# Three narrow products in place of one wide and one narrow product per weight block, with new places for the split weights

## The chip, the cores and the metric

One core of one Trainium2 chip. The metric is the device time of one execution in microseconds (us), the median of several runs; the kernel before takes 1187.89 us (1187.58 to 1189.35 in 3 runs).

## What is computed

A decoder block of width 1024 over 256 tokens, batch 1, in float32, followed by a second block of another kind. The first has two layers; each is a feed-forward, a mixing step and another feed-forward. Cut to what matters:

```
def swiglu(x, w_gate, w_up, w_down):          # D_MODEL 1024, D_FF 2816
    return (silu(x @ w_gate) * (x @ w_up)) @ w_down

for layer in range(2):
    h = h + 0.5 * swiglu(rms_norm(h, g1), w_gate1, w_up1, w_down1)
    hn = rms_norm(h, mix_norm_g)
    # layer 0: hn @ a_w_in, a causal convolution of 31 taps, layer_norm; memory attention
    # layer 1: hn @ b_w_in, causal attention with 12 heads; memory attention
    h = h + concat(primary, mem_out) @ w_o
    h = h + 0.5 * swiglu(rms_norm(h, g2), w_gate2, w_up2, w_down2)
# second block: rms_norm(h) @ w_in_2 (some 6,700 columns), a differential attention, an mLSTM,
# gates, @ w_a_2, @ w_b_2, @ w_out_2, a norm, and the sum with h
```

There are four feed-forwards, numbered 0 to 3 below. They hold about three fifths of all multiplications.

## The kernel before

**Exact products from rounded ones.** TensorE multiplies in a rounded float32 (`fp32r`). Each operand is therefore split into a rounded part and the rest: a weight w into `whi` + `wlo`, an activation x into `xh` + `xl`. A product is then the sum of three: hi·xh, hi·xl and lo·xh, added up in PSUM.

**Weights in slots.** All weights come in 403 slots of 128 partitions by 1024 values (512 KB), in the order of use. SyncE's queue loads slot i into `raw[i % 7]`; ScalarE writes its rounded half to `whi[i % 5]` (line 1253), VectorE the rest to `wlo[i % 5]` (line 1864). ScalarE may write slot i once TensorE has used slot i - 5 (semaphore `used`). In a slot for columns there are 4 pieces of 128 rows by 256 columns; each piece is two blocks of 128 by 128.

**Three forms of product**, all issued by the helper `mm` (line 509):
- *Wide* (`two_blocks`, feed-forwards alone). The activations are laid out as [piece, hi or lo, 256 tokens], so that xh and xl of a piece lie next to each other. For each block one matmul of 512 columns multiplies hi by [xh | xl] into a whole PSUM bank, and one of 256 columns adds lo·xh to the bank's left half. A pair of blocks (256 output features) takes two banks, and the result is the sum of each bank's two halves. ScalarE copies the right halves to SBUF (`half`, line 1295), VectorE adds the left halves (`halves`, line 1913).
- *Narrow* (`pair` and `direct`, the other matrices whose result has the features on the partitions: slots 72 to 75, 78 to 85, 90 to 97, 258 to 265, 334 to 350, 371 to 394, which are 69 slots). For each block three matmuls of 256 columns, hi·xh, hi·xl and lo·xh, into one half of a bank. Both blocks of a pair share one bank and there is nothing to add up.
- *Rows* (`rows_steps`, `query_rows`). The activations are the stationary operand, and the weights move through TensorE, 512 or 256 columns at a time.

**Order of a feed-forward** (`ffn`). For p = 0 to 10 (256 columns of the hidden layer): the gate product over 8 pieces (2 slots) into banks 0 and 1, then the up product into banks 2 and 3. TensorE waits for `sum` of the pair before, before it overwrites a pair of banks. ScalarE and VectorE follow a slot at a time: right halves, sum, scale by the norm's row (`gate_scale`, line 2006), SiLU, product gate by up (line 2014), and the split of the product into `gh` and `gl` of the tile `g`. Then for p = 0 to 3 the down product over 22 pieces (6 slots) into banks 4 and 5, 6 and 7, 0 and 1, 4 and 5, its sum of halves, the scale, the sum with h, and the split of the new h into the activations of the next step (`prep`).

**Places in SBUF.** This is about a place's address in a partition, modulo 256 bytes. The tiles `whi` and `wlo` begin at one and the same place, called 0 here, and a slot's stride is 4096 bytes, so every block of every slot begins at 0. `activations` makes two views on each tile `x0`, `x1`: `xh`, `xl` begin at +64, `rh`, `rl` at 0. The feed-forwards' and the narrow products' moving operands (`xh`, `xl`) are at +64, and so is the tile `g` of feed-forwards 0, 1 and 3; `g` of feed-forward 2 is at +128. Rows products have rh, rl (0) in the slots 28 to 31, 86 to 89, 234 to 257 and 395 to 402, and xh, xl (+64) in 76, 77 and in 351 to 370.

Of the kernel before, what the change touches and what calls it, by code (L numbers as in the profile page):

```python
# [15 lines left out]
S = 256  # L16
# [16 lines left out]
SLOTS = 403  # L33

# [43 lines left out]
def a_slot(p):  # L78

    return AIN + 4 * p + (2 if p else 0)  # L80

# [113 lines left out]
def buffers(nc, ctx):  # L195
# [9 lines left out]
    B.whi = sb("whi", [128, SPLIT, SLOT], F32R)  # L205
    B.wlo = sb("wlo", [128, SPLIT, SLOT], F32R)
# [3 lines left out]
    B.diag = sb("diag", [128, 2, 128])  # L210
# [21 lines left out]
    B.ln1 = sb("ln1", [128, 128])  # L232
# [36 lines left out]
    A.cv = sb("cv", [128, 6, S], F32, mx)  # L269
    A.sg = sb("sgm", [128, 2, 512], F32, mx)  # L270
# [19 lines left out]
    sb("even", [128, 4], F32, kv)  # L290
# [25 lines left out]
    T.ctap = sb("ctap", [128, 8, 4], F32, mx)  # L316
# [7 lines left out]
    T.ptbuf = sb("pt2", [128, 2, 256], F32, mx)  # L324
    T.lamr = T.ptbuf[:, 0, :].rearrange("p (a d) -> p a d", a=4)
# [8 lines left out]
def signals(nc, ctx):  # L334
# [17 lines left out]
    sums = []  # L352
    for f in range(4):
        for p in range(PAIRS):
            sums += [("gate", f, p), ("up", f, p)]
        sums += [("down", f, p) for p in P4]


# [15 lines left out]
    s.consts = sig("consts", ["ones", "ident", "ln1", "upper", "identb", "mask", "half", "alib", "ident4"])  # L374
# [72 lines left out]
    s.half = sig("right_half", sums)  # L447


    s.sum = sig("halves_sum", sums)  # L450
# [52 lines left out]
def tensor_engine(nc, B, s):  # L503
    pe = nc.tensor
    bank, psum, xh, xl, rh, rl, ident, ones = B.bank, B.psum, B.xh, B.xl, B.rh, B.rl, B.ident, B.ones
# [5 lines left out]
    def weights(i, nk, n):  # L511
        h = B.whi[:, i % SPLIT, 0:nk * n].rearrange("p (k n) -> p k n", k=nk)
        l = B.wlo[:, i % SPLIT, 0:nk * n].rearrange("p (k n) -> p k n", k=nk)
        return h, l
# [15 lines left out]
    def two_blocks(b, h, l, x, start, stop, ready=None):  # L530


        two_rounded(b, h, x, start)
        if ready is not None:
            pe.wait_ge(*ready)
        return two_left(b, l, x, stop)
# [10 lines left out]
    def part(x, slot, b, ks, start, stop, gen=None, between=None):  # L547
# [8 lines left out]
        for i, kc in enumerate(ks):  # L556
            k = kc % 4
            if slot == 0 and i == 2:
                pe.wait_ge(*s.hi.at(0))
            if between and i == 2:  # L560
                between()
            if gen:
                first_use(s.x_hi, gen, kc)
                first_use(s.x_lo, gen, kc)
            if late:
                two_rounded(b, h[:, k, :], x[:, kc], start and i == 0)
            else:
                t = two_blocks(b, h[:, k, :], l[:, k, :], x[:, kc], start and i == 0, stop and kc == ks[-1], ready.get(i))
        if late:
            pe.wait_ge(*s.lo.at(slot))  # L570
            for kc in ks:
                t = two_left(b, l[:, kc % 4, :], x[:, kc], stop and kc == ks[-1])
# [126 lines left out]
    def ffn(f, x, gen):  # L699
        base, F = FFN[f], B.ffn[f]  # L700
        for p in range(PAIRS):
            if f == 0 and p == LATE:
                rows((rh[1], rl[1]), "mem0", 8, MKV0, 512, [[4], [5]])
            if p:
                pe.wait_ge(*s.sum.at(("gate", f, p - 1)))
            elif f == 1:
                pe.wait_ge(*s.h.at((2, 0)))
            elif f == 2:
                pe.wait_ge(*s.h.at((3, 2)))
            elif f == 3:  # L710
                pe.wait_ge(*s.h.at((5, 0)))
            if p:
                cols(x, 8, up_slot(f, p), 0)
                pe.wait_ge(*s.sum.at(("up", f, p - 1)))
                cols(x, 8, up_slot(f, p) + 2, 2)
            else:
                part(x, base, 0, range(4), True, False, gen)
                if f in (1, 3):
                    pe.wait_ge(*s.h.at((2, 2) if f == 1 else (5, 1)))
                elif f == 2:  # L720
                    pe.wait_ge(*s.sum.at(("up", 1, PAIRS - 1)))
                part(x, base + 1, 2, range(4), True, False)
                part(x, base + 2, 0, range(4, 8), False, True, gen)
                part(x, base + 3, 2, range(4, 8), False, True)
        for p in range(4):
# [4 lines left out]
            if p == 2:  # L730
                pe.wait_ge(*s.sum.at(("gate", f, PAIRS - 1)))
# [4 lines left out]
    def down(f, F, slot, b, first):  # L736
        i = slot
        for k0 in range(0, 22, 4):
# [4 lines left out]
            for k in range(m):  # L743
# [4 lines left out]
                t = two_blocks(b, h[:, k, :], l[:, k, :], F.g[:, kc], kc == 0, kc == 21, s.lo.at(i) if k == 0 else None)  # L748
# [45 lines left out]
    def conv_mean(c):  # L794
# [5 lines left out]
        v = flat(B.diag[:]) if c is None else MA.cv[:, c, :]  # L800
        return mm(bank[4][:, 0:S], B.ln1[:], v, c == CONV_PE[0], c == CONV_PE[-1])

    def mix_a():
# [3 lines left out]
        pe.wait_ge(*s.sum.at(("up", 0, PAIRS - 1)))  # L807
# [207 lines left out]
    def gate_cols():  # L1015
# [5 lines left out]
        for k in range(8):  # L1021
            t = direct(bank[5][:, 0:S], h[:, k, :], l[:, k, :], 0, k, k == 0, k == 7, i if k == 0 else None)
# [14 lines left out]
    def rest():  # L1037
        for i in range(3):
            if i:
                pe.wait_ge(*s.zo_act.at(i - 1))  # L1040
            yield from rows_steps((xh[0], xl[0]), None, 8, ZO2 + 4 * i, 512, [[6], [7]], first=i,
                                  free=s.zo_dve.at(i - 1) if i else None)
        for c in range(16):
# [7 lines left out]
            for k in range(8):  # L1051
                t = direct(bank[6 + c % 2][:, 0:S], h[:, k, :], l[:, k, :], 0, k, k == 0, k == 7, i if k == 0 else None)
# [52 lines left out]
    def second():  # L1105
        X0 = (xh[0], xl[0])
        pe.wait_ge(*s.sum.at(("up", 3, PAIRS - 1)))
        pair(0, 0, QK2, 2, range(4), True, False, "w2")
# [1817 lines left out]
```

## Time and profile before

| | |
|---|---|
| median of 3 runs | 1187.89 us |
| profiled execution, span | 1186.7 us |
| TensorE busy | 1179.2 us, 99% |
| its weight loads (PEld) | 1043.9 us, 88% |
| VectorE busy | 862.0 us, 73% |
| ScalarE busy | 677.7 us, 57% |
| DMA queues' share of 16 engines | 55.9% |
| TensorE's granted clock | 1.000 |

The profiled execution's span lies 1.2 us under the median of the runs. A matmul's duration in the profile is modelled up to the end of its pipeline, and matmuls overlap: a 256-column matmul shows 276 to 280 ns although one starts every 113 to 118 ns. Rates are therefore read from the starts in the timeline and not from the mean durations. The timeline merges consecutive instructions of one form into one row with their count; the first matmul of a row starts at the row's time.

### The profile page before, as it was taken

The page shows a single profiled execution, that of the slowest core. Times are in us where ns is not written, and L with a number is a line of the kernel's source. Part 1 is how long each engine was busy: PE and PEld are TensorE (multiplying, and loading weights), DVE is VectorE, ACT ScalarE, POOL GpSimd, SP SyncE. Part 2 cuts the span into 40 slices and gives each one's busy share as a digit, 9 for nine tenths or more (in the row PEclk, how much of TensorE's full clock was granted, in tenths as well). Part 3 has the DMA queues.
Part 4 walks back from the last instruction along what each step waited for, and adds up shares of the span by engine and source line. Part 5 has one row for each costly group of instructions (what it writes and reads, how often), then busy time and mean ns, then how long its engine had stood idle before and what let it go on. Part 6 is the DMA issues. An engine that isn't in the chain of part 4 may idle for free.

```text
span 1186.7 us, 18987 instructions
## 1 busy us (share of the span) xinstructions
PE 1179.2 (99%) x7592; PEld 1043.9 (88%) x7592; DVE 862.0 (73%) x1213; ACT 677.7 (57%) x1036; POOL 65.5 (6%) x86
## 2 busy tenths in 40 slices
PE   9999999999999999999999999999999999999998
PEld 8888889969988888888888888998888899879996
DVE  7977766886887767787766677677776668666875
ACT  6766644547665555655554457566554545566463
POOL 1501000200010000000000022000000000000000
PEclk9999999999999999999999999999999999999999
DMA  8865656664656656656655553256655665536450
GB/s 305 305 195 180 194 176 204 210 174 137 202 189 187 190 173 195 202 172 212 192 173 173 190 177 125 74 194 193 192 184 178 194 215 173 185 125 184 144 171 35
DMA packets 65398, 215.85 MB, mean 182 GB/s; under 512 B 8352, under 2 KB 12064, under 8 KB 65184
## 3 DMA queue, kind: packets, MB, share of 16 engines
q1 hardware_dynamic: 62608, 210.64, 55.5%
q10 hardware_dynamic: 2704, 4.02, 1.0%
q8 instruction: 60, 0.98, 0.3%
q14 instruction: 26, 0.21, 0.1%
HBM read 212.70 MB, written 1.93 MB: 181 GB/s over the span
## 4 chain that ended last, share of the span: by engine, by line
PE 97%; DVE 1%; DMA 1%; ACT 0%; issue 0%; SPq 0%; POOL 0%; DVEq 0%; POOLq 0%
PE psum L509 96%; DMA raw<-in_slots 1%; PE psum L920 0%; DVE small L2308 0%; PE psum L1062 0%; ACT whi L1253 0%; PE psum L880 0%; PE psum L970 0%; PE psum L1011 0%; PE psum L1203 0%; PE psum L673 0%; DVE qkc L2678 0%; DVE wlo L1864 0%; PE psum L956 0%; ACT vn L1637 0%
## 5 line engine op out<-in xcount | busy, mean ns | idle before, releaser
L509 PE MATMUL psum<-x,whi 128*128 128x512 f32 (+1 forms) x2512 | 633.2, 343 | 0.2 <-DVE x L1935 0.2
L1864 DVE TENSOR_TENSOR wlo<-raw,whi 128x1024 fp32r<-128x1024 f32 (+2 forms) x402 | 474.2, 1191 | 162.1 <-ACT whi L1253 159.1
L1253 ACT CAST whi<-raw 128x1024 fp32r<-128x1024 f32 (+2 forms) x402 | 405.4, 1022 | 156.0 <-PE psum L509 151.2
L509 PE MATMUL psum<-x,wlo 128*128 128x256 f32 x1960 | 430.7, 279 | 0.0
L509 PEld LDWEIGHTS psum<-x,wlo 128*128 128x128 f32 x1960 | 366.7, 188 | 58.2 <-DVE wlo L1980 0.4
L509 PEld LDWEIGHTS psum<-x,whi 128*128 128x128 f32 x2512 | 382.1, 188 | 2.3 <-issue 1.2
L509 PE MATMUL psum<-g,whi 128*128 128x512 f32 x704 | 218.7, 392 | 0.0
L509 PEld LDWEIGHTS psum<-g,wlo 128*128 128x128 f32 x704 | 132.2, 188 | 29.5
L509 PE MATMUL psum<-whi,x 128*128 128x512 f32 (+1 forms) x512 | 140.6, 375 | 0.0
L509 PE MATMUL psum<-g,wlo 128*128 128x256 f32 x704 | 139.2, 279 | 0.0
L509 PEld LDWEIGHTS psum<-g,whi 128*128 128x128 f32 x704 | 106.8, 188 | 0.0
L509 PEld LDWEIGHTS psum<-whi,x 128*128 128x128 f32 x512 | 89.1, 188 | 16.1 <-DVE zob L2444 0.2
L509 PE MATMUL psum<-wlo,x 128*128 128x512 f32 (+1 forms) x256 | 86.1, 372 | 0.0
L1295 ACT COPY pr<-psum 128x512 f32<-128x512 f32 x44 | 25.8, 586 | 61.6 <-PE psum L509 61.5
L1295 ACT COPY gr<-psum 128x512 f32<-128x512 f32 x44 | 25.7, 585 | 60.9 <-PE psum L509 60.8
L1913 DVE TENSOR_TENSOR pr<-psum,pr 128x512 f32<-128x512 f32 x44 | 30.4, 691 | 35.3 <-ACT pr L1295 35.3
L1913 DVE TENSOR_TENSOR gr<-psum,gr 128x512 f32<-128x512 f32 x44 | 30.4, 691 | 32.2 <-ACT gr L1295 32.2
L509 PEld LDWEIGHTS psum<-wlo,x 128*128 128x128 f32 x256 | 45.8, 188 | 8.9
L1327 ACT ACTIVATE x<-first 128x256 fp32r<-128x256 f32 x64 | 28.6, 500 | 43.7 <-DVE first L2064 29.2
L1935 DVE SCALAR_TENSOR_TENSOR x<-first,x 128x256 fp32r<-128x256 f32 x64 | 28.0, 484 | 21.8 <-ACT x L1327 21.7
L1396 ACT ACTIVATE gr<-gr 128x512 f32<-128x512 f32 x44 | 27.7, 633 | 22.8 <-DVE gr L2006 22.3
L1405 ACT CAST g<-pr 128x512 fp32r<-128x512 f32 x44 | 27.4, 622 | 18.9 <-DVE pr L2014 18.6
(317 smaller groups left out, 775.6 us busy)
## 6 DMA issues: line engine op xcount, KB each, us to landing
raw<-in_slots SPq DMA_DIRECT2D x371, 512.0 KB, 4.2
raw<-in_slots SPq DMA_DIRECT2D x16, 384.0 KB, 3.3
raw<-in_slots SPq DMA_DIRECT2D x16, 256.0 KB, 2.9
h<-conv_mem SPq DMA_DIRECT2D x8, 284.0 KB, 5.0
mkv<-in_mem ACTq DMA_DIRECT2D x1, 1024.0 KB, 12.4
memt<-in_mem_cols ACTq DMA_DIRECT2D x1, 1024.0 KB, 15.7
conv_mem<-hc SPq DMA_DIRECT2D x3, 288.0 KB, 2.2
h<-conv_mem SPq DMA_DIRECT2D x4, 142.0 KB, 2.9
```

The costliest lines, as they stand in the source:

```text
L509: return pe.matmul(o, l, r, start=start, stop=stop, skip_group_check=True)
L1253: act.copy(held(B.whi[:, i % SPLIT, :], *n), held(B.raw[:, i % RAW, :], *n)).then_inc(*s.hi.now(i))
L1295: act.copy(out, psum[:, b:b + 2, S:2 * S]).then_inc(*s.half.now(key))
L1327: act.activation(x[:, c, :], hT[:, c, :], ACT.Copy, scale=gcol[:, c, gi:gi + 1]).then_inc(*s.x_hi.now((gen, c)))
L1396: act.activation(r, r, ACT.Silu).then_inc(*s.silu.now((f, p)))
L1405: act.copy(F.gh[:, 2 * p:2 * p + 2, :], in_pairs(F.pr[:, p % 2, :])).then_inc(*s.g_hi.now((f, p)))
L1864: dve.tensor_tensor(held(B.wlo[:, i % SPLIT, :], *n), held(B.raw[:, i % RAW, :], *n), held(B.whi[:, i % SPLIT, :], *n).bitcast(F32), ALU.s ...
L1913: dve.tensor_tensor(out, psum[:, b:b + 2, 0:S], out, ALU.add).then_inc(*s.sum.now(key))
L1935: dve.scalar_tensor_tensor(out=l[:, c, :], in0=hT[:, c, :], scalar=gcol[:, c, gi:gi + 1], in1=h[:, c, :].bitcast(F32), op0=ALU.mult, op1=A ...
```

## The change

In the feed-forwards each block gets three products of 256 columns, and both blocks of a pair go to the halves of one bank (`block`). `half`, `halves` and their semaphores go away: VectorE scales the gate and multiplies by the up product straight from PSUM. Gate and up products alternate between two banks each (three in feed-forward 0, where the norm's row comes late), and TensorE waits for a bank two pairs back.

A slot of `whi` and `wlo` gets 32 more values (128 bytes) of stride, so that the beginnings of the five places alternate between 0 and +128; since five odd strides also separate the two tiles, `wlo` of a slot lies at +128 where `whi` lies at 0 and the other way round. In rows slots (`EVEN`) the extra 128 bytes bring both back to 0. In the narrow slots 334 to 350 and 371 to 386 (`SHIFTED`) both are 64 bytes further on, and the activations of the second block move from xh[0], xl[0] to rh[0], rl[0] (+64 to 0), here called `xh[2]`, `xl[2]`. `even` grows by 64 bytes, which moves `g` of feed-forward 2 from +128 to +192. To make room, `diag` and `ln1` move into the space of the mixing step and `ctap` into `ptbuf`.

```diff
+def hi_slot(B, i):
+    r = i % SPLIT
+    o = 16 if i in SHIFTED else BESIDE if i in EVEN and r % 2 else 0
+    return B.whi[:, r, o:o + SLOT]
+
+def lo_slot(B, i):
+    r = i % SPLIT
+    o = 16 if i in SHIFTED else BESIDE if i in EVEN and r % 2 == 0 else 0
+    return B.wlo[:, r, o:o + SLOT]
...
-    B.whi = sb("whi", [128, SPLIT, SLOT], F32R)
-    B.wlo = sb("wlo", [128, SPLIT, SLOT], F32R)
+    B.whi = sb("whi", [128, SPLIT, SLOT + BESIDE], F32R)
+    B.wlo = sb("wlo", [128, SPLIT, SLOT + BESIDE], F32R)
...
-    sb("even", [128, 4], F32, kv)
+    sb("even", [128, 20], F32, kv)
...
-    def two_rounded(b, h, x, start):
-        for j in range(2):
-            mm(bank[b + j], h[:, j * 128:(j + 1) * 128], x.rearrange("p a b -> p (a b)"), start, False)
-    def two_left(b, l, x, stop):
-        for j in range(2):
-            t = mm(bank[b + j][:, 0:S], l[:, j * 128:(j + 1) * 128], x[:, 0, :], False, stop)
-        return t
+    def block(b, h, l, x, start, stop, ready=None):
+        for j in range(2):
+            o, q = bank[b][:, j * S:(j + 1) * S], slice(j * 128, (j + 1) * 128)
+            mm(o, h[:, q], x[:, 0, :], start and j == 0, False)
+            mm(o, h[:, q], x[:, 1, :], False, False)
+            if ready is not None and j == 0:
+                pe.wait_ge(*ready)
+            t = mm(o, l[:, q], x[:, 0, :], False, stop)
+        return t
...
+        gates, ups = ((0, 1, 6), (2, 3, 7)) if f == 0 else ((0, 1), (2, 3))
...
-            if p:
-                pe.wait_ge(*s.sum.at(("gate", f, p - 1)))
+            if p >= turns:
+                pe.wait_ge(*s.gate.at((f, p - turns)))
...
-                pe.wait_ge(*s.sum.at(("up", f, p - 1)))
-                cols(x, 8, up_slot(f, p) + 2, 2)
+                if p >= turns:
+                    pe.wait_ge(*s.mul.at((f, p - turns)))
+                cols(x, 8, up_slot(f, p) + 2, u)
...
-    def half(key, slot, out, b):
-        act.wait_ge(*s.used.at(slot))
-        act.copy(out, psum[:, b:b + 2, S:2 * S]).then_inc(*s.half.now(key))
...
-    def halves(key, out, b):
-        dve.wait_ge(*s.half.at(key))
-        dve.tensor_tensor(out, psum[:, b:b + 2, 0:S], out, ALU.add).then_inc(*s.sum.now(key))
-        dve.wait_ge(*s.sum.at(key))
...
-            dve.tensor_tensor(r, r, row, ALU.mult).then_inc(*s.gate.now((f, p)))
+            dve.wait_ge(*s.used.at(up_slot(f, p) + (1 if p else 2)))
+            dve.tensor_tensor(in_pairs(F.gr[:, p % 2, :]), in_pairs(bank[gates[p % len(gates)]]), row, ALU.mult).then_inc(
+                *s.gate.now((f, p)))
...
-            halves(("down", f, p), tmp, (4, 6, 0, 4)[p])
-            dve.scalar_tensor_tensor(out=tmp, in0=tmp, scalar=0.5, in1=row, op0=ALU.mult, op1=ALU.mult).then_inc(
+            dve.wait_ge(*s.used.at(down_slot(f, p) + 5))
+            dve.scalar_tensor_tensor(out=tmp, in0=in_pairs(bank[(4, 6, 0, 4)[p]]), scalar=0.5, in1=row, op0=ALU.mult, op1=ALU.mult).then_inc(
```

## Rows read from the trace of the kernel before

**Rows 1.** The page: span, busy shares, and the chain's shares.
```profile
span 1186.7 us, 18987 instructions
PE 1179.2 (99%) x7592; PEld 1043.9 (88%) x7592; DVE 862.0 (73%) x1213; ACT 677.7 (57%) x1036; POOL 65.5 (6%) x86
...
PE 97%; DVE 1%; DMA 1%; ACT 0%; issue 0%; SPq 0%; POOL 0%; DVEq 0%; POOLq 0%
```
**Rows 2.** Waits of TensorE, the longest: total us, times, longest us.
```profile
PE psum L509 <- POOL ones L2702: 1.0, 1, 1.0
```
**Rows 3.** Groups by shape: xcount, then busy us, mean ns, idle before.
```profile
L509 PE MATMUL psum<-x,whi 128*128 128x512 f32 x1408 | 437.0, 392 | 0.2 <-DVE x L1935 0.2
L509 PE MATMUL psum<-g,whi 128*128 128x512 f32 x704 | 218.7, 392 | 0.0
L509 PE MATMUL psum<-x,whi 128*128 128x256 f32 x1104 | 196.3, 280 | 0.0
```
**Rows 4.** Timeline of TensorE, feed-forward 2 (start us, us): four blocks between.
```profile
520.08 0.62 PE L509 MATMUL psum<-x,whi 128*128 128x512 f32 x2
...
521.46 0.62 PE L509 MATMUL psum<-x,whi 128*128 128x512 f32 x2
```
**Rows 5.** Timeline of TensorE, down product of feed-forward 2: four blocks between.
```profile
639.79 0.62 PE L509 MATMUL psum<-g,whi 128*128 128x512 f32 x2
...
641.18 0.62 PE L509 MATMUL psum<-g,whi 128*128 128x512 f32 x2
```
**Rows 6.** Timeline of TensorE, narrow slots 334 to 336: 24 blocks between.
```profile
962.72 0.40 PE L509 MATMUL psum<-x,whi 128*128 128x256 f32 x2
...
971.20 0.50 PE L509 MATMUL psum<-ones,acc 128*128 128x4 f32 x4
```
**Rows 7.** Timeline of TensorE, narrow slots 72 to 74 (24 blocks) and into 75.
```profile
201.67 0.39 PE L509 MATMUL psum<-x,whi 128*128 128x256 f32 x2
...
209.83 0.50 PE L509 MATMUL psum<-ones,acc 128*128 128x4 f32 x4
...
210.63 0.40 PE L509 MATMUL psum<-x,whi 128*128 128x256 f32 x2
...
210.99 0.40 PE L509 MATMUL psum<-x,whi 128*128 128x256 f32 x2
```
**Rows 8.** Timeline of TensorE, narrow slots 78 to 83 (48 blocks), then into 84.
```profile
218.82 0.39 PE L509 MATMUL psum<-x,whi 128*128 128x256 f32 x2
...
235.14 0.60 PE L777 MATMUL psum<-ident,sqb 128*128 128x128 f32 x4
...
239.72 0.40 PE L509 MATMUL psum<-x,whi 128*128 128x256 f32 x2
...
240.07 0.40 PE L509 MATMUL psum<-x,whi 128*128 128x256 f32 x2
```
**Rows 9.** Timeline of TensorE in narrow slot 380: one block between.
```profile
1111.40 0.39 PE L509 MATMUL psum<-x,whi 128*128 128x256 f32 x2
...
1111.74 0.39 PE L509 MATMUL psum<-x,whi 128*128 128x256 f32 x2
```
**Rows 10.** Timeline of TensorE, rows slot 243: six matmuls of 512 between.
```profile
691.03 1.07 PE L509 MATMUL psum<-whi,x 128*128 128x512 f32 x4
...
692.39 1.07 PE L509 MATMUL psum<-whi,x 128*128 128x512 f32 x4
```
**Rows 11.** Timeline of TensorE, rows slots 352 and 353: three matmuls of 512 between.
```profile
1017.45 0.63 PE L509 MATMUL psum<-whi,x 128*128 128x512 f32 x2
...
1018.15 0.63 PE L509 MATMUL psum<-whi,x 128*128 128x512 f32 x2
```
**Rows 12.** Timeline of VectorE and of ScalarE, feed-forward 2, around one gate sum.
```profile
568.64 0.59 ACT L1295 COPY gr<-psum 128x512 f32<-128x512 f32 x1 [1.70 <-PE psum L509]
...
569.26 0.69 DVE L1913 TENSOR_TENSOR gr<-psum,gr 128x512 f32<-128x512 f32 x1 [1.07 <-ACT gr L1295]
569.98 0.69 DVE L2006 TENSOR_TENSOR gr<-gr,rowr 128x512 f32<-128x512 f32 x1
```

More of the change, by code:

```diff
@@ L33 @@
 SLOTS = 403
+BESIDE = 32
+SHIFTED = {*range(QK2, VB2), *range(GAB2, WA2)}
+EVEN = {*range(MKV0, MKV0 + 4), *range(QMEM, QMEM + 2), *range(MKV1, MKV1 + 4), *range(KLIN, WO1), *range(VB2, GAB2),
+        *range(OUT2, SLOTS)}
 NORM = ((5, 5), (75, 4), (101, 4), (169, 4), (237, 0), (269, 6), (337, 4))
@@ L269, in buffers @@
     A.cv = sb("cv", [128, 6, S], F32, mx)
+    A.ln1 = sb("ln1", [128, 128], F32, mx)
+    A.diag = sb("diag", [128, 2, 128], F32, mx)
     A.sg = sb("sgm", [128, 2, 512], F32, mx)
@@ L373, in signals @@
     s.w4_first = sig("conv_weights_first", CONV_PE[:1])
-    s.consts = sig("consts", ["ones", "ident", "ln1", "upper", "identb", "mask", "half", "alib", "ident4"])
+    s.consts = sig("consts", ["ones", "ident", "upper", "identb", "mask", "half", "alib", "ident4"])
     s.fills = sig("fills", ["hc", "freq", "qk"])
@@ L720, in ffn @@
                 elif f == 2:
[L721 to L724, printed above, removed]
+                    pe.wait_ge(*s.mul.at((1, PAIRS - 1)))
+                part(x, base + 1, u, range(4), True, False)
+                part(x, base + 2, g, range(4, 8), False, True, gen)
+                part(x, base + 3, u, range(4, 8), False, True)
         for p in range(4):
@@ L730, in ffn @@
             if p == 2:
-                pe.wait_ge(*s.sum.at(("gate", f, PAIRS - 1)))
+                pe.wait_ge(*s.gate.at((f, PAIRS - 1)))
             if p == 3:
@@ L1252, in split_to @@
                 act.wait_ge(*s.used.at(i - SPLIT))
-            act.copy(held(B.whi[:, i % SPLIT, :], *n), held(B.raw[:, i % RAW, :], *n)).then_inc(*s.hi.now(i))
+            act.copy(held(hi_slot(B, i), *n), held(B.raw[:, i % RAW, :], *n)).then_inc(*s.hi.now(i))
             splits[0] += 1
@@ L1863, in split_to @@
             dve.wait_ge(*s.hi.at(i))
-            dve.tensor_tensor(held(B.wlo[:, i % SPLIT, :], *n), held(B.raw[:, i % RAW, :], *n),
-                              held(B.whi[:, i % SPLIT, :], *n).bitcast(F32), ALU.subtract).then_inc(*s.lo.now(i))
+            dve.tensor_tensor(held(lo_slot(B, i), *n), held(B.raw[:, i % RAW, :], *n),
+                              held(hi_slot(B, i), *n).bitcast(F32), ALU.subtract).then_inc(*s.lo.now(i))
             splits[0] += 1
@@ L2183, in mix_a @@
         some(cd, 100)
-        part = flat(B.diag[:])
+        part = flat(MA.diag[:])
         dve.wait_ge(*s.pe_norm.at((1, "row")))
@@ L2761, in gpsimd_engine @@
     pool.wait_ge(*s.used.at(AIN - 1))
+    pool.memset(MA.ln1[:], 1.0 / 768)
     pool.memset(MA.hc[:, :, 0:30], 0.0)
```

132 lines of the change are left out of this document (54 added, 78 removed).

## The prediction, made before the changed kernel ran

> **What bounds the kernel now.** I read the page's busy shares and the chain that ended last first: TensorE is busy for 1179.2 of 1186.7 us, and 97% of the chain is TensorE [rows 1]. Then its waits, where the longest is 1.0 us, at the very start [rows 2]. So neither VectorE, ScalarE nor the weight stream sets the time. What is left is the rate at which TensorE starts matmuls. Its busy time does not tell that, since matmuls overlap; the timeline's starts do. The question of the whole change is one number: how long a block of 128 by 128 weights takes as two matmuls (512 + 256 columns) and how long as three (256 each). Both forms are in the trace of before, and so the answer can be read.
>
> *Wide form.* In feed-forward 2 the rows at 520.08 and 521.46 have four blocks between them, 1.38 us or 345 ns a block [rows 4]. The down product of feed-forward 2, whose `g` lies at +128 and not at +64, takes 1.39 us for four, 347.5 ns [rows 5]. Feed-forwards hold 1408 + 704 = 2112 blocks [rows 3].
>
> *Narrow form.* Here the trace shows two speeds for the same instructions. Slots 334 to 336: 971.20 - 962.72 = 8.48 us for 24 blocks, 353 ns [rows 6]. Slots 72 to 74: 209.83 - 201.67 = 8.16 us for 24 blocks, 340 ns [rows 7]. Slots 78 to 83: 16.32 us for 48, again 340 ns [rows 8]. Slot 380: 0.34 us for one [rows 9], and 381 to 384 likewise. The narrow slots hold 1104 / 2 = 552 blocks, 8 in each of 69 [rows 3]. So 14 of the 69 run at 340 ns (113.3 per matmul), the other 55 at about 353.5 (118 per matmul). A stretch keeps its speed until something interrupts it: after the four small matmuls at 209.83 the next block takes 0.36 us [rows 7], and after the convolution at 235.14 the blocks go at 0.35 [rows 8], although form and places are what they were. The clock is at its upper level throughout, so this is not the clock.
>
> *Do places matter?* Rows products say yes. With the stationary operand at 0 and the weights at 0, six matmuls of 512 columns take 1.36 us, 226.7 ns each [rows 10]. With the stationary operand at +64, three take 0.70 us, 233.3 each [rows 11]. 226.7 for 512 and 113.3 for 256 columns are the same time per column, 0.4427 ns. I read this as the floor (nothing in the trace repeats faster), and what lies above it as the price of reading the moving operand and loading the next weights from SBUF at once.
>
> The Trainium skill says the opposite. "SBUF — State Buffer", section "Who interferes with whom", gives TensorE two independent read ports, one for the moving operand and one for weight loads, and states that TensorE never waits on anyone. The two rates of one form in rows 10 and 11, and in rows 6 and 7, disagree with it, so I go by the rows. "TensorE: Matmul & The Clock Gate", section "Back-to-back issue gap", gives N/2.4 + 2.5 ns: 109.2 ns for 256 and 215.8 for 512 columns. By that a block costs 327.5 narrow against 325.0 wide, and the change would be an estimated 5.3 us slower. No row reaches those figures (113.3 and 226.7 are the lowest).
>
> **The change part by part.**
>
> 1. *Feed-forwards from wide to narrow.* The number of columns is the same (768), the weight loads go from two to three a block. At the floor a block takes 340 ns. 2112 - 176 = 1936 blocks (the 176 are the down product of feed-forward 2) gain 5 ns each, 9.7 us [rows 4, 7]; the 176 gain 7.5 each, 1.3 us [rows 5]. At the slow speed 1936 blocks lose 8.5 each, 16.5 us, and the 176 lose 6, 1.1 us [rows 6]. The bounds are thus -11.0 and +17.6 us, and the new places decide between them.
>
> 2. *The new places for narrow products.* Before, every moving operand is 64 bytes from every stationary one. After, hi and lo of a slot lie in opposite halves of 256 bytes and swap with each slot, so the distance is +64 for one and -64 for the other. No narrow row of before has -64 or an alternation. Bounds: all 440 slow blocks (55 slots) go to the floor, 440 x 13.5 = 5.9 us gained; or the 112 fast ones fall to the slow speed, 1.5 us lost. I take the floor for this and for point 1. Reasons: the floor is reached by this very form with a weight load every 256 columns, in three separate stretches [rows 7 to 9]; what differs between a fast and a slow stretch can only be when the two reads meet, and a slow stretch lasts as long as each instruction repeats the last one's meeting. With two distances in each block it can't repeat from one matmul to the next. This is an argument, not a row, and it carries most of the doubt.
>
> 3. *VB2, VA2, ZO2 (slots 351 to 370).* Their stationary operand moves from +64 to 0, the weights stay at 0: the case of rows 10. 20 slots x 12 matmuls x (233.3 - 226.7) ns = 1.6 us gained. This part has an exact precedent. Other rows slots keep their places.
>
> 4. *No halves, no sums.* 104 copies of 0.59 us leave ScalarE and 104 sums of 0.69 us leave VectorE [rows 12], some 61 and 72 us. Off the path: worth 0. Each was waiting for TensorE (1.70 us) or for ScalarE (1.07 us) when its turn came. `gate_scale` reads PSUM instead of SBUF at the same 0.69 us as the sum that did. The wait for `used` that moves from ScalarE to VectorE has the splits of later slots queued behind it, as it had on ScalarE; they are made four slots ahead, which covers it.
>
> 5. *Banks and waits of TensorE.* Before, it needed the sum of the pair before, some 2 slots after that product's end. Now it needs `gate` or `mul` of two pairs back, 4 slots or more later at about 2.7 us a slot. Neither shows in the waits now [rows 2], and I see none coming: 0. If VectorE's chain were late, 40 waits of some 0.1 us would be 4 us.
>
> 6. *The wider slots, `diag`, `ln1`, `ctap`:* places alone. `ln1` is set later by GpSimd, well before its use: 0.
>
> Sum: -9.7 - 1.3 - 5.9 - 1.6 = -18.5 us on a span of 1186.7, or 1168.2; the median lies 1.2 us over the span, which gives **1169.4 us**.
>
> **The rivals.**
>
> *The places don't help* (20%). The narrow form stays at 353.5 ns in all 2664 blocks. That gives +17.6 + 1.5 - 1.6 = +17.5 us: **1205.4 us**, slower. This also is what follows if places do not matter and the speed is set by chance at each start, but with all the luck gone. For: 55 of 69 slots are slow now, among them the long stretches after an uninterrupted feed-forward [rows 6]. Against: rows 10 and 11. It decides from the point where a narrow block's mean passes 345 ns. (The skill's rule on ports, named above, would put the change here: nothing is gained by a place.)
>
> *Mixed* (18%). Some stretches or slots fast, others slow, or all at something between. From 1169.4 to 1205.4 the time is linear in the slow share; it equals the time of before at 51% slow. With shares of 20 to 80% that is 1177 to 1198 us, and I put 11 of the 18 on faster, 2 on the same, 5 on slower. For: speed changed at interruptions in all three fast stretches, and feed-forwards have such (norm sums and row turns between slots, as at 209.83).
>
> *A new wait* (5%). TensorE at the floor, but held by `gate` or `mul`, or by weights that must now be split every 2.72 us and not 2.76: the 4 us of point 5 up to 20, 1173 to 1190 us. For: TensorE is faster, and VectorE splits 1024 values and does the hidden layer's work. Against: it loses 72 us of work, more than the 18 that the span shrinks.
>
> **How the numbers follow.** The sum's case has 57%. Its own range is 1164 to 1175: below, if interrupted stretches lose less than now; above, if a sixth of the blocks stay slow. A measurement of this kernel tells 0.2% or 2.4 us from no change. Faster by more: 57 + 11 + 3 = 71%. Within: 2 + 1 = 3%. Slower: 20 + 5 + 1 = 26%. The range that should hold 8 in 10 takes in the sum's case, the mixed one and the new wait and leaves out the first rival: 1164 to 1200.
>
> **What the profile after would show.** Right: in any feed-forward the timeline's narrow rows (x,whi x2, x,wlo x1) start every 0.34 us; likewise in slots 334 to 350; matmuls of slots 351 to 370 start every 0.227; TensorE's waits stay at the start; VectorE's busy time falls by some 70 us, ScalarE's by 60. Wrong in the main step: rows every 0.353 or 0.354 in feed-forwards, and a span over 1200. Wrong in point 5: a wait of TensorE for VectorE at line 2006's or 2014's successor, repeated every pair.

## The result and the profile after

| | before | after |
|---|---|---|
| median of 4 runs | 1188.36 us (1187.58 to 1189.35) | 1172.05 us (1171.85 to 1172.12) |
| ratio after to before, 95% interval | | 0.9861 [0.9847, 0.9875] |
| profiled execution, span | 1186.7 us | 1170.7 us |

The change makes the kernel 16.3 us faster; the spans of the two profiled executions differ by 16.0 us. Forecast were 18.5 us and 1169.4 us.

The page of after (against [rows 1] and [rows 3]): span, busy times, shares of the chain that ended last, and two groups by shape (count, then busy us, mean ns, idle before).
```profile
span 1170.7 us, 22956 instructions
PE 1163.0 (99%) x9704; PEld 1117.5 (95%) x9704; DVE 797.1 (68%) x1109; ACT 620.8 (53%) x932; POOL 62.1 (5%) x86
...
PE 97%; DVE 1%; DMA 1%; ACT 0%; issue 0%; SPq 0%; POOL 0%; DVEq 0%; POOLq 0%
...
L519 PE MATMUL psum<-x,whi 128*128 128x256 f32 x3920 | 671.7, 277 | 0.3 <-DVE x L1925 0.3
...
L519 PE MATMUL psum<-g,whi 128*128 128x256 f32 x1408 | 239.6, 276 | 0.0
```
TensorE issues 9704 matmuls and not 7592, in less time. It is still 97% of the chain. VectorE lost 64.9 us of busy time (862.0 to 797.1), ScalarE 56.9 (677.7 to 620.8).

Waits of TensorE in after, the first two of the list (total us, times, longest us), against [rows 2]:
```profile
PE psum L519 <- POOL ones L2692: 1.0, 1, 1.0
PE psum L519 <- DVE x L1925: 0.3, 1, 0.3
```
The others of the list are of 0.3 us or less, and none is for `gate` or `mul`.

TensorE's timeline in feed-forward 2 of after (start us, us), against [rows 4]:
```profile
481.20 0.39 PE L519 MATMUL psum<-x,whi 128*128 128x256 f32 x2
...
487.32 0.50 PE L519 MATMUL psum<-ones,acc 128*128 128x4 f32 x4
488.12 0.40 PE L519 MATMUL psum<-x,whi 128*128 128x256 f32 x2
...
490.26 0.40 PE L519 MATMUL psum<-x,whi 128*128 128x256 f32 x2
```
From 481.20 to 487.32 there are 18 blocks: 6.12 us, 340 ns a block, where the wide form took 345. Then four small matmuls of the norm come in between, and from 488.12 to 490.26 six blocks take 2.14 us, 357 ns each. This is the slow speed. It lasts through slots 169 and 170; from the fourth block of slot 171 on they take 340 again. The same two speeds are found in the whole trace. I call a narrow slot slow if a matmul of 256 columns starts in it every 118 ns at the median, and fast at 113 to 114. Of the 341 narrow slots 14 are slow: 0, 5, 32, 75, 84, 85, 90, 169, 170, 269, 270, 376, 378 and 386. Before, 55 of 69 were slow.

TensorE's timeline in the down product of feed-forward 2, against [rows 5], and in slots 334 to 336, against [rows 6]:
```profile
637.25 0.39 PE L519 MATMUL psum<-g,whi 128*128 128x256 f32 x2
...
637.59 0.39 PE L519 MATMUL psum<-g,whi 128*128 128x256 f32 x2
```
```profile
950.72 0.40 PE L519 MATMUL psum<-x,whi 128*128 128x256 f32 x2
...
958.90 0.50 PE L519 MATMUL psum<-ones,acc 128*128 128x4 f32 x4
```
0.34 us for one block, where it was 347.5 ns (the first 15 whole blocks after the start of this down product, in slots 210 and 211, take 340 each); and 24 blocks in 8.18 us, 341 ns each, where it was 353. In rows slot 353, against [rows 11]:
```profile
1003.68 0.62 PE L519 MATMUL psum<-whi,x 128*128 128x512 f32 x2
...
1004.36 0.62 PE L519 MATMUL psum<-whi,x 128*128 128x512 f32 x2
```
Three matmuls of 512 columns in 0.68 us, 226.7 ns each, where it was 233.3.

Where the 16.0 us went, by sections (time from a section's first matmul to the next slot's first behind it, out of the starts in both timelines):

| section | before, us | after, us | difference |
|---|---|---|---|
| feed-forward 0 (slots 0 to 27, 32 to 71) | 184.58 | 182.12 | -2.46 |
| feed-forward 1 | 183.37 | 180.75 | -2.62 |
| feed-forward 2 | 183.50 | 180.52 | -2.98 |
| feed-forward 3 | 182.92 | 180.51 | -2.41 |
| slots 90 to 97 | 22.78 | 22.14 | -0.64 |
| slots 258 to 265 | 23.58 | 22.78 | -0.80 |
| slots 334 to 341 | 23.28 | 22.55 | -0.73 |
| slots 343 to 350 | 23.03 | 22.22 | -0.81 |
| slots 351 to 358 (VB2, VA2) | 23.67 | 23.12 | -0.55 |
| slots 359 to 370 (ZO2) | 43.48 | 43.04 | -0.44 |
| slots 371 to 386 | 57.32 | 56.77 | -0.55 |
| slots 387 to 394 | 23.14 | 22.34 | -0.80 |

The feed-forwards give 10.5 us, the narrow slots elsewhere 4.3 (with 0.11 gained in slot 342 and 0.11 lost in slots 72 to 85), slots 351 to 370 give 1.0.

### The profile page after: what moved, and what is told of

Its sections match the earlier page's. It is cut to its first block, busy times and chain, and to the rows that moved or that the text cites. A ratio compares the mean times of both kernels' runs of the same rounds, so it can differ in the third digit from the quotient of the medians.

```text
span 1170.7 us, 22956 instructions
## 1 busy us (share of the span) xinstructions
PE 1163.0 (99%) x9704; PEld 1117.5 (95%) x9704; DVE 797.1 (68%) x1109; ACT 620.8 (53%) x932; POOL 62.1 (5%) x86
## 4 chain that ended last, share of the span: by engine, by line
PE 97%; DVE 1%; DMA 1%; ACT 0%; issue 0%; SPq 0%; POOL 0%; DVEq 0%; POOLq 0%
PE psum L519 95%; DMA raw<-in_slots 1%; PE psum L936 0%; DVE small L2298 0%; PE psum L1078 0%; ACT whi L1269 0%; PE psum L896 0%; PE psum L1027 0%; PE psum L1219 0%; PE psum L986 0%; PE psum L685 0%; DVE qkc L2668 0%; DVE wlo L1860 0%; PE psum L972 0%; ACT vn L1633 0%
## 5 line engine op out<-in xcount | busy, mean ns | idle before, releaser
L519 PE MATMUL psum<-x,whi 128*128 128x256 f32 x3920 | 671.7, 277 | 0.3 <-DVE x L1925 0.3
L519 PEld LDWEIGHTS psum<-x,whi 128*128 128x128 f32 x3920 | 589.6, 188 | 1.4 <-issue 0.9
L519 PE MATMUL psum<-x,wlo 128*128 128x256 f32 x1960 | 538.3, 276 | 0.0
L519 PE MATMUL psum<-g,whi 128*128 128x256 f32 x1408 | 239.6, 276 | 0.0
L519 PEld LDWEIGHTS psum<-g,whi 128*128 128x128 f32 x1408 | 211.7, 188 | 0.0
L519 PE MATMUL psum<-g,wlo 128*128 128x256 f32 x704 | 194.3, 276 | 0.0
L2006 DVE TENSOR_TENSOR pr<-gr,psum 128x512 f32<-128x512 f32 x44 | 30.2, 687 | 14.7 <-PE psum L519 13.7
L1998 DVE TENSOR_TENSOR gr<-psum,rowr 128x512 f32<-128x512 f32 x44 | 30.0, 689 | 14.3 <-PE psum L519 14.3
L2728 POOL TENSOR_TENSOR small<-small,mhalf 128x2 f32<-128x2 f32 x7 | 7.6, 1084 | 478.0 <-DVE small L1904 478.0
L2011 DVE TENSOR_TENSOR g<-pr,g 128x512 fp32r<-128x512 f32 x44 | 31.2, 708 | 0.7 <-ACT g L1412 0.7
```

Source lines behind the costliest of these rows:

```text
L519: return pe.matmul(o, l, r, start=start, stop=stop, skip_group_check=True)
L1998: dve.tensor_tensor(in_pairs(F.gr[:, p % 2, :]), in_pairs(bank[gates[p % len(gates)]]), row, ALU.mult).then_inc(*s.gate.now((f, p)))
L2006: dve.tensor_tensor(F.pr[:, p % 2, :], F.gr[:, p % 2, :], bank[ups[p % len(ups)]], ALU.mult).then_inc(*s.mul.now((f, p)))
L2011: dve.tensor_tensor(F.gl[:, 2 * p:2 * p + 2, :], in_pairs(F.pr[:, p % 2, :]), F.gh[:, 2 * p:2 * p + 2, :].bitcast(F32), ALU.subtract).then ...
L2728: pool.tensor_tensor(small[:, c0 + 2:c0 + 4], small[:, c0:c0 + 2], B.mhalf[:, 0:2], ALU.pow).then_inc(*s.rstd.now(("n", n)))
```

## The experiments

My theory after the result was that of the prediction: the narrow form is fast only with the new places, and two distances in each block keep it from repeating a bad meeting of the two reads. Each kernel is named by its difference to the changed kernel, except the second. Times are medians; ratios are to the kernel before on the same chip. In all of them the granted clock is 0.999 or 1.000.

**The form without the places.** All slots of `whi` and `wlo` begin at 0, `even` and the second block's activations are where they were.
```diff
 def hi_slot(B, i):
-    o = 16 if i in SHIFTED else BESIDE if i in EVEN and r % 2 else 0
+    o = 0
...
-    B.whi = sb("whi", [128, SPLIT, SLOT + BESIDE], F32R)
+    B.whi = sb("whi", [128, SPLIT, SLOT], F32R)
...
-    sb("even", [128, 20], F32, kv)
+    sb("even", [128, 4], F32, kv)
```
(likewise `lo_slot` and `wlo`; `xh[2]`, `xl[2]` become `xh[0]`, `xl[0]`)

> The changed kernel with every place put back: narrow feed-forwards, no sums of halves, but hi and lo of every slot at 0 modulo 256, the second block's activations at +64, g of feed-forward 2 at +128. Theory 'swap' (a narrow stretch keeps its speed of 340 or 353 ns a block as long as the places repeat from slot to slot; only the change of halves between slots ends a slow stretch): long slow stretches in the feed-forwards at 353 ns, slots 334 to 350 back at 353, slots 351 to 370 back at 233 ns a matmul; 1190 to 1206 us, at least 1 us slower than the kernel before. Rival 'places are idle' (the speed of a stretch is luck): feed-forwards at 340 as in the changed kernel, 1172 to 1180 us.

Measured: 1199.41 us (1197.70 to 1203.92), ratio 1.0096 [1.0068, 1.0123]. Slower than before. TensorE's timeline in feed-forward 2 of this kernel:
```profile
520.26 0.40 PE L519 MATMUL psum<-x,whi 128*128 128x256 f32 x2
...
528.74 0.40 PE L519 MATMUL psum<-x,whi 128*128 128x256 f32 x2
```
24 blocks in 8.48 us: 353 ns. 293 of 341 narrow slots are slow, in long runs (90 to 233, 269 to 343). Yet slots 7 to 27 are fast, with one distance, +64, in every matmul. So one distance does not make a stretch slow. It has both speeds, and keeps the one it has over many slots.

**The places without the form.** The kernel before, with wide feed-forwards, and all new places.
```diff
+    o = 16 if i in SHIFTED else BESIDE if i in EVEN and r % 2 else 0
+    return B.whi[:, r, o:o + SLOT]
...
+    B.whi = sb("whi", [128, SPLIT, SLOT + BESIDE], F32R)
+    B.wlo = sb("wlo", [128, SPLIT, SLOT + BESIDE], F32R)
```

> The kernel before with the new places alone: wide feed-forwards and sums of halves as they were. Theory 'swap': narrow slots outside the feed-forwards go from 353 to 340 ns a block as in the changed kernel (4.3 us gained there) and slots 351 to 370 gain 1.0 us. The wide form's reaction to the places is not known: its block stays at 345 ns (1183 us in all), with bounds of 340 (1172 us, which would mean that the narrow form added nothing to the places) and 347.5 (1188 us). Rival 'places are idle': 1188 us with the narrow slots at 353.

Measured: 1193.01 us (1192.95 to 1193.18), ratio 1.0038 [1.0023, 1.0053]. The 69 narrow slots did as expected: 7 are slow. The miss is the wide form. TensorE's timeline in feed-forward 2 of this kernel, with 22 blocks between:
```profile
520.05 0.62 PE L530 MATMUL psum<-x,whi 128*128 128x512 f32 x2
...
527.75 0.63 PE L530 MATMUL psum<-x,whi 128*128 128x512 f32 x2
```
7.70 us, 350 ns a block, where it was 345 [rows 4]. The places that are good for the narrow form cost the wide one 5 ns a block. Hence neither half of the change pays alone (+11.0 and +4.6 us against the kernel before), and both together give -16.3.

**hi and lo in the same half, both swapping from slot to slot.** Each block has one distance again.
```diff
 def lo_slot(B, i):
-    o = 16 if i in SHIFTED else BESIDE if i in EVEN and r % 2 == 0 else 0
+    o = 16 if i in SHIFTED else 0 if i in EVEN and r % 2 else BESIDE
```

> The changed kernel, but in the narrow slots other than 334 to 350 and 371 to 386 lo lies in the same half of 256 bytes as hi; both still swap halves from slot to slot. Theory 'swap': as the changed kernel, 1172 us within 1.5, slow blocks only behind interruptions. Rival 'opposite halves' (what counts is that hi and lo of one slot lie in opposite halves): slow stretches in the feed-forwards as in the kernel with the old places, over 1185 us.

Measured: 1173.55 us (1173.20 to 1174.21), ratio 0.9875 [0.9860, 0.9890]. 32 narrow slots are slow, never more than four in a row (2 to 5). Two distances in a block are therefore not what makes it fast. Nor does every swap end a slow stretch. TensorE's timeline in the down product of feed-forward 2 of this kernel, from slot 210 on:
```profile
600.59 0.40 PE L519 MATMUL psum<-g,whi 128*128 128x256 f32 x2
...
606.24 0.39 PE L519 MATMUL psum<-g,whi 128*128 128x256 f32 x2
...
608.97 0.39 PE L519 MATMUL psum<-g,whi 128*128 128x256 f32 x2
```
16 blocks in 5.65 us, 353 ns, through slots 210 and 211, so also through the swap between them; 8 blocks in 2.73 us, 341 ns, in slot 212. The first swap moves hi from 64 bytes above the moving operand (`g` at +192, taken modulo 256) to 64 below, the second from below to above. It is so wherever in this kernel a slow stretch meets a swap with no other work of TensorE between (slots 1 to 4 left out, since in slots 1 to 3 all hi products come before the lo products): the three swaps from above to below, into slots 79, 102 and 211, leave it slow, and the twelve from below to above, into 46, 81, 212 and 261 among others, end it within a block. In the changed kernel the swaps into 6, 33, 91 and 377, all from below to above, end one within two blocks.

**hi always at 0, lo always at +128.** Two distances in a block, no swap between slots.
```diff
-    o = 16 if i in SHIFTED else BESIDE if i in EVEN and r % 2 else 0
+    o = 16 if i in SHIFTED else BESIDE if r % 2 else 0
...
-    o = 16 if i in SHIFTED else BESIDE if i in EVEN and r % 2 == 0 else 0
+    o = 16 if i in SHIFTED else BESIDE if (r % 2 == 0) == (i in EVEN) else 0
```

> The changed kernel, but in the narrow slots other than 334 to 350 and 371 to 386 hi always lies at 0 and lo always at +128: opposite halves in each slot, no swap from slot to slot. Theory 'swap': a stretch that an interruption leaves slow stays so to the next interruption, so feed-forwards 2 and 3 or others have runs of tens of slots at 353 ns; 1180 to 1200 us. Rival 'opposite halves': as the changed kernel, 1172 us within 1.5, no slow run longer than two slots.

Measured: 1177.76 us (1177.33 to 1178.70), ratio 0.9911 [0.9896, 0.9926]. 57 slots are slow, now in long runs: 5 to 27, 32 to 44, 258 to 268. Feed-forward 0 of this kernel, slots 12 to 14:
```profile
40.19 0.40 PE L519 MATMUL psum<-x,whi 128*128 128x256 f32 x2
...
48.75 0.40 PE L519 MATMUL psum<-x,whi 128*128 128x256 f32 x2
```
24 blocks in 8.56 us, 357 ns, with two distances in every block. This refutes the prediction's reason directly. The three long runs end at other work on TensorE (rows products after 27, transposes before 45, the norm's sums before 269), but such work does not always end one: the norm's transposes between slots 6 and 7 lie inside the first. In the changed kernel, with the swap, no run is longer than two slots.

**Distances of 0 and 128 bytes.** Every feed-forward slot 64 bytes on, so that hi or lo begins where the moving operand begins, or 128 bytes from it. Instructions and swap are those of after.
```diff
-SHIFTED = {*range(QK2, VB2), *range(GAB2, WA2)}
+SHIFTED = {*range(0, MKV0), *range(MKV0 + 4, AIN), *range(FFN[1], KLIN), *range(FFN[3], VB2), *range(GAB2, WA2)}
```

> The changed kernel with the weights of all four feed-forwards 64 bytes further on: their moving operand then begins 0 or 128 bytes from the stationary one, not 64 on either side; opposite halves and the swap stay. Theory 'swap alone': the distance does not matter, 1172 us within 1.5, as slow runs end at each swap anyway. Rival 'distance': blocks of the feed-forwards stay above 340 ns also far from interruptions (the wide form at distance 128 took 347.5 ns where at 64 it took 345), 1177 us or more.

Measured: 1205.52 us (1204.91 to 1205.68), ratio 1.0146 [1.0129, 1.0163]. All 272 feed-forward slots are slow. Feed-forward 2 of this kernel:
```profile
520.29 0.40 PE L519 MATMUL psum<-x,whi 128*128 128x256 f32 x2
...
528.83 0.40 PE L519 MATMUL psum<-x,whi 128*128 128x256 f32 x2
```
24 blocks in 8.54 us, 356 ns. 64 bytes cost 33.5 us. At distances of 64 bytes a stretch of the narrow form can be fast; at 0 and 128 none was. This is so for the narrow form only: rows products with both operands at 0 start every 227 ns at the median in slots 28 to 31 and 395 to 402 of the kernel before, and every 233 in slots 351 to 370, 64 bytes apart.

The Trainium skill gives TensorE two independent read ports and says that it never waits on anyone ("SBUF — State Buffer", section "Who interferes with whom"). If nothing but independent ports counted, a place would cost nothing; this pair of kernels has the same instructions, no wait of TensorE over 1.0 us, and takes 1205.5 against 1172.05 us. Whether TensorE waits there for a read of its own or for something else, no run shows.

**The removed work given back.** ScalarE copies a finished bank (256 columns of each block, as many values as the right halves had) and VectorE adds the bank to the copy, ahead of the operations that read PSUM; 104 of each; what they write is overwritten.
```diff
+            halves(("gate", f, p), in_pairs(F.gr[:, p % 2, :]), gates[p % len(gates)])
             dve.tensor_tensor(in_pairs(F.gr[:, p % 2, :]), in_pairs(bank[gates[p % len(gates)]]), row, ALU.mult).then_inc(
```

> The changed kernel with the 104 copies from PSUM of 0.59 us back on ScalarE and the 104 sums of 0.69 us back on VectorE, each ahead of the instruction that takes its place now (which overwrites the result). Theory 'off the path': 1172 us within 1, with VectorE's busy time up by 72 us and ScalarE's by 61. Rival 'the lighter engines gave part of the gain': 3 us slower or more, with waits of TensorE for VectorE in the feed-forwards.

Measured: 1172.80 us (1172.51 to 1173.96), ratio 0.9872 [0.9857, 0.9887]. The page of this kernel, then its longest wait of TensorE:
```profile
span 1170.9 us, 23300 instructions
...
PE 1163.2 (99%) x9704; PEld 1117.4 (95%) x9704; DVE 858.1 (73%) x1213; ACT 673.0 (57%) x1036; POOL 61.7 (5%) x86
```
```profile
PE psum L525 <- POOL ones L2730: 1.0, 1, 1.0
```
VectorE is busy 61.0 us more than in after, ScalarE 52.2, and feed-forwards 1 to 3 have the same lengths to 0.01 us. So the 113 us of removed work are worth 0.8 us at most, within the intervals of the two ratios, and the gain is TensorE's rate.

**A swap at every slot.** Five places in a ring leave one pair without a swap: places 4 and 0 both begin at 0. It is there that slots 84 and 85, 169 and 170, 269 and 270 are slow in pairs in after. Here the place goes by the slot's number.
```diff
-    o = 16 if i in SHIFTED else BESIDE if i in EVEN and r % 2 else 0
+    o = 16 if i in SHIFTED else BESIDE if (r if i in EVEN else r + i) % 2 else 0
...
-    o = 16 if i in SHIFTED else BESIDE if i in EVEN and r % 2 == 0 else 0
+    o = 16 if i in SHIFTED else BESIDE if (r + 1 if i in EVEN else r + i) % 2 else 0
```

> The changed kernel with places by the slot's number and not by its place in the ring of five, so that the halves also swap from the ring's fifth place to its first (narrow slots other than 334 to 350 and 371 to 386). Theory 'swap': slots 85, 170 and 270, which are slow behind a slow slot in the ring's fifth place, become fast, those in front of them (84, 169, 269) stay slow; 0.3 us less, too little for the times. Rival 'interruptions alone decide': 85, 170 and 270 stay slow, or others do.

Measured: 1171.49 us (1171.08 to 1171.69), ratio 0.9859 [0.9844, 0.9873]. TensorE's timeline in slots 84 and 85, first of after, then of this kernel:
```profile
237.21 0.40 PE L519 MATMUL psum<-x,whi 128*128 128x256 f32 x2
...
242.21 0.40 PE L519 MATMUL psum<-x,whi 128*128 128x256 f32 x2
```
```profile
237.35 0.40 PE L519 MATMUL psum<-x,whi 128*128 128x256 f32 x2
...
239.49 0.40 PE L519 MATMUL psum<-x,whi 128*128 128x256 f32 x2
...
239.85 0.39 PE L519 MATMUL psum<-x,whi 128*128 128x256 f32 x2
...
242.23 0.39 PE L519 MATMUL psum<-x,whi 128*128 128x256 f32 x2
```
In after 14 blocks in 5.00 us, 357 ns, over both slots. Here 6 blocks in 2.14 us, 357 ns, up to slot 85, and from the swap on 7 blocks in 2.38 us, 340 ns. Nothing else comes between: this swap, of hi from 64 bytes below the moving operand to 64 above, ends the slow speed. But slots 5, 75, 169 and 269 are fast from their start, which a swap does not explain. In this kernel hi is at +128 in them, 64 bytes above the moving operand, and in after at 0, 64 below. Slot 5 tells little: it is fast too in the kernel with the work given back and in the next one, where its places are those of after.

**KLIN and VLIN with the swap.** Most of their rows products take 230 to 241 ns for 512 columns; would a swap bring the floor?
```diff
-EVEN = {*range(MKV0, MKV0 + 4), *range(QMEM, QMEM + 2), *range(MKV1, MKV1 + 4), *range(KLIN, WO1), *range(VB2, GAB2),
+EVEN = {*range(MKV0, MKV0 + 4), *range(QMEM, QMEM + 2), *range(MKV1, MKV1 + 4), *range(QLIN, VLIN), *range(VB2, GAB2),
```

> The changed kernel with the new alternating places also in the rows slots of 768 columns (234 to 241 and 250 to 257), whose matmuls take 230 to 241 ns for 512 columns and 113 to 120 for 256 although both operands begin at 0. If what holds for the narrow form holds for rows, these 16 slots go to 226.7 and 113.3 ns and some 1.4 us are gained (1170.7 us); if a fixed place is better for rows, they get slower (up to 2 us).

Measured: 1172.40 us (1171.82 to 1172.44), ratio 0.9866 [0.9851, 0.9880]. KLIN takes 17.16 us and not 17.29, VLIN 47.28 and not 47.31. Neither expectation came: the two sections keep their lengths to 0.13 us.

**hi always at +128, lo always at 0.** The mirror of the no-swap kernel: hi 64 bytes above the moving operand.
```diff
-    o = 16 if i in SHIFTED else BESIDE if i in EVEN and r % 2 else 0
+    o = 16 if i in SHIFTED else BESIDE if (r % 2 == 1) == (i in EVEN) else 0
...
-    o = 16 if i in SHIFTED else BESIDE if i in EVEN and r % 2 == 0 else 0
+    o = 16 if i in SHIFTED else BESIDE if r % 2 == 0 else 0
```

> The changed kernel with the mirror image of the run without a swap: hi always at +128, lo always at 0 (narrow slots other than 334 to 350 and 371 to 386), opposite halves, no swap from slot to slot. Theory 'side': in the changed kernel and in the one with a swap at every slot, the slots that come out slow behind small matmuls (5, 75, 84, 90, 169, 269) are those with hi at 0, 64 bytes below the moving operand, and those with hi at +128, 64 bytes above it, come out fast; so nearly no slow slot outside 334 to 386, and 1170 to 1171 us. Theory 'swap alone': as the run without a swap, 1178 us, with slow runs of up to 23 slots.

Measured: 1174.15 us (1174.07 to 1175.39), ratio 0.9877 [0.9862, 0.9891]. Slots 5, 75, 84, 90, 169 and 269 are all fast, without any swap. 29 slots are slow, and 24 of them are the whole down product of feed-forward 2, whose `g` at +192 lies above hi. TensorE's timeline at its begin:
```profile
599.00 0.39 PE L519 MATMUL psum<-x,whi 128*128 128x256 f32 x2
...
599.34 0.40 PE L519 MATMUL psum<-g,whi 128*128 128x256 f32 x2
...
607.54 0.40 PE L519 MATMUL psum<-g,whi 128*128 128x256 f32 x2
```
The last `x` block starts the first `g` block 0.34 us later; the next 23 take 8.20 us, 357 ns each. Nothing interrupts TensorE there. What changes is the moving operand's place, and with it the speed.

**hi and lo both always at +128.** If the side of hi alone decided, this would be as fast.
```diff
-    o = 16 if i in SHIFTED else BESIDE if i in EVEN and r % 2 else 0
+    o = 16 if i in SHIFTED else BESIDE if (r % 2 == 1) == (i in EVEN) else 0
...
-    o = 16 if i in SHIFTED else BESIDE if i in EVEN and r % 2 == 0 else 0
+    o = 16 if i in SHIFTED else BESIDE if (r % 2 == 0) == (i in EVEN) else 0
```

> As the kernel with the old places in the feed-forwards, mirrored: hi and lo of every narrow slot (other than 334 to 350 and 371 to 386) both at +128, nothing swaps and nothing is opposite. Theory 'side of hi decides': feed-forwards at 340 ns a block, 1170 to 1173 us. Theory 'side of each': the stretch is as slow as with both at 0, since what keeps a stretch slow is that all three products of a block meet alike; 1190 to 1200 us.

Measured: 1191.62 us (1185.68 to 1192.94), ratio 1.0020 [1.0008, 1.0031]. 208 slots are slow, among them 101 to 168 and 269 to 333; 45 to 74 and 169 to 209 are fast. The theory falls as I had put it: the side of hi decides only where lo is on the other side. With one half for both and no swap there are both speeds again, in long runs, as in the first experiment. One of its ten executions took 1185.68 us and the others 1191.39 or more, so that the speeds of stretches can differ between executions of one kernel.

**The changed kernel once more**, on the chip of the two kernels above.

> The changed kernel itself, on the same chip as the two others, as the measure for them: 1172 us within 0.5.

Measured: 1172.05 us (1171.79 to 1172.19), ratio 0.9856 [0.9842, 0.9871]. The same time; but which slots are slow is not wholly fixed by the places. In this trace slots 1 and 92 are slow and slot 0 is not. Slots 32, 75, 84, 85, 90, 169, 170, 269, 270, 376, 378 and 386 are slow in both traces of the changed kernel and in that with the work given back.

**hi always at +128, lo at 0, and `g` of feed-forward 2 at +64.**
```diff
-    sb("even", [128, 20], F32, kv)
+    sb("even", [128, 52], F32, kv)
```
(on top of the kernel with hi at +128)

> The kernel with hi always at +128 and lo at 0, and with g of feed-forward 2 moved by 128 bytes to +64, where the other feed-forwards have theirs. Theory 'side' (a block is safe where its moving operand begins 64 bytes below hi, at risk where it begins 64 bytes above): the 24 slots 210 to 233, slow in the kernel without this move since their g lay at +192, above hi, run at 340 ns; 2.6 us less than that kernel, 1171.5 us within 0.5, so slightly under the changed kernel. Rival 'the down product of feed-forward 2 is slow for another reason': 1174 us as before the move.

Measured: 1171.63 us (1171.18 to 1172.44), ratio 0.9857 [0.9840, 0.9873]. As expected. The same down product in this kernel:
```profile
599.57 0.39 PE L519 MATMUL psum<-g,whi 128*128 128x256 f32 x2
...
605.69 0.39 PE L519 MATMUL psum<-g,whi 128*128 128x256 f32 x2
```
18 blocks in 6.12 us, 340 ns. Only slots 376, 378 and 386 are slow; there hi is at +192 and the moving operand at 0, which is 64 below again. The ratios of this kernel, of the one with a swap at every slot and of the changed one overlap in their intervals; neither is shown to beat the changed kernel.

## Why the prediction was right, and which step of it was not

The four arrangements at a distance of 64 bytes, narrow form:

| | places swap from slot to slot | no swap |
|---|---|---|
| hi and lo in opposite halves | 1172.05 (14 slow slots) | 1177.76 (57; hi below x); 1174.15 (29; hi above x, but for one `g`) |
| hi and lo in the same half | 1173.55 (32) | 1199.41 (293; at 0); 1191.62 (208; at +128) |

(The 1199.41 lacks the second block's new places too. These are worth at most the 4.0 us that slots 334 to 394 gained, so that the cell would be at least 1195.4.)

- *What bounds the kernel.* Right. TensorE's rate set the time before and after, and handing back 113 us of other engines' work left feed-forwards 1 to 3 at the same length.
- *Point 1, the form in the feed-forwards.* Right: 340 ns a block in feed-forward 2 and in its down product. -10.5 us against -11.0. The 7 slow slots there (0, 5, 32, 169, 170, 269, 270) are 56 blocks at 17 ns, an estimated 0.95 us, more than is missing. Four of them are measured: in the kernel with hi at +128 and `g` moved, where 169, 170, 269 and 270 are fast, feed-forwards 2 and 3 are 0.26 and 0.25 us shorter.
- *Point 2, the places, size.* -4.3 us against -5.9. Seven slots outside the feed-forwards stay slow (0.8 us at 13.5 ns a block). The rest is spread: where 8 slow slots became fast and 0.86 us were due, sections gained 0.73 to 0.81. Behind small matmuls the first block still takes some 440 ns and the next one to three up to 359 (slot 337: 435, 359, 356, then 340).
- *Point 2, its reason.* Wrong, and this is the step that failed: "With two distances in each block it can't repeat from one matmul to the next". Slow stretches with two distances in each block last 23 slots where the places do not swap (slots 5 to 27 at hi 0, lo +128), and two slots in after where the ring's places 4 and 0 do not. With one distance a block and a swap, no stretch is longer than four slots. What the runs show in its place is that a stretch can keep its speed over tens of slots with the same places, slow or fast; that a swap which brings hi from 64 bytes below the moving operand to 64 above ends the slow one (at slot 85), while the opposite swap left it slow in all three places where it met one (into 79, 102 and 211 with both in the same half); that in after fast stretches pass through all swaps unharmed; and that hi above and lo below the moving operand mostly keeps work behind an interruption fast, where the other way round it is often slow. That the number came out is in part luck: the reason asks for two distances in each block and nothing else, so it would have given the same 1169.4 us for the kernel without the swap, which took 1177.76, and no such gain for the one with one distance a block, which took 1173.55. The change happened to have the swap as well.
- *Point 3, VB2, VA2, ZO2.* -1.0 us against -1.6. 226.7 ns for 512 columns holds in most of VB2 and VA2 (rows slot 353 above), which gained 0.55 us of the 0.63 that 8 slots were due. In ZO2 attention matmuls come in between; there half of the matmuls still take 228 to 236 ns, and it gained 0.44 of 0.95.
- *Point 4, halves and sums.* Right at 0, by the run that gave them back. VectorE's busy time fell by 65 us and ScalarE's by 57, not 72 and 61.
- *Point 5, banks and waits.* Right at 0: no wait of TensorE over 0.3 us but at the start, and none for `gate` or `mul`.
- *The rivals.* "The places don't help" names a state that exists: it is what the narrow form does at its old places (+11.0 us) and at distances of 0 and 128 bytes, 1205.5 us. That the forecast for this rival had been 1205.4 is chance: it had 353.5 ns in all narrow blocks, and here those of the feed-forwards take 356 and most others are fast. Its premise, that a place changes nothing, is what fell. "Mixed" is true in kind, with 14 slow slots of 341. By the formula of the Trainium skill's "TensorE: Matmul & The Clock Gate", section "Back-to-back issue gap", which the section gives for a matmul in isolation, the change would have cost an estimated 5.3 us; the lowest that repeats in after is 113.3 ns for 256 columns and 226.7 for 512, not 109.2 and 215.8, and one of 512 takes as long as two of 256, so that no cost of the third matmul of a block is seen.

Not settled: why there are two speeds. That the two reads meet in SBUF is argued; no row shows it, and the wide form and the rows products prefer other places. Not tested is whether 256 bytes is the period that counts: all places here differ by multiples of 64 bytes within 256. That the accesses of other engines play a part is not ruled out, though 113 us more of their work changed no length of feed-forwards 1 to 3. Nor is the rule complete: slot 92, whose hi is at 0, starts late in after (554 ns for its first block) and is fast, and is slow in the second trace of the same kernel. Shown are the speeds, and which changes of place moved them in these kernels.

## What to carry to other kernels

Where TensorE bounds a kernel, read the start-to-start time of each form of matmul in several stretches; two speeds of the same instructions mean that something outside them, here the operands' places modulo 256 bytes, is worth tuning. For blocks of three narrow products as here, place the two stationary operands 64 bytes to either side of the moving one and not 0 or 128 from it, and either keep the more used one above or let the places swap often. Try the places anew for every other form: the wide form lost with these, and rows products did better with both operands at one place. Test a form together with its layout: each half of this change alone made the kernel slower.

## What the runs showed of the hardware that I had not expected

- Two speeds for one instruction stream at one clock: a 256-column matmul with a weight load every 113.3 or every 118 ns. The slow speed is 353 ns a block where hi and lo lie in the same half and 357 where they lie in opposite ones. A speed can last over long stretches (slots 5 to 27 with hi always at 0, some 66 us), and it changed at interruptions and at changes of places, though not at each.
- The place of the moving operand against the stationary one: at 0 and 128 bytes all 272 feed-forward slots were slow (356 ns a block in feed-forward 2), at 64 bytes 265 of them took 340.
- The wide form reacts the other way: 345 ns a block with all weights at one place, 350 with alternating ones.
- Rows products of 512 columns: 227 ns with both operands at one place, 233 with 64 bytes between them.
- At the fast speed a third weight load costs nothing: 3 matmuls of 256 columns with 3 loads take 340 ns, 2 (512 and 256) with 2 loads 345.
